# Second layer: scores within groups of four tokens from products on VectorE, summed in 32 by 32 blocks

## The reference, cut to what matters

```
u = rms_norm(h);  q, f, i, gate = split(u @ w_in);  q = silu(q)
f = lb + (1 - lb) * sigmoid(f);  k = 1 - f
S_t = diag(f_t) S_{t-1} + k_t i_t^T;  o_t = S_t^T q_t        (per head)
h + (rms_norm(o) * silu(gate)) @ w_out
```

## Time and profile before

| | |
|---|---|
| median of the runs | 1182.67 us |
| the profiled execution | 1182.29 us |
| its span | 1180.6 us |
| PE busy | 1169.3 us (99%) |
| DVE busy | 784.2 us (66%) |
| ACT busy | 419.6 us (36%) |
| POOL busy | 148.9 us (13%) |

### The profile page before, as it was taken

How to read it: one execution, slowest core, us unless ns; L and a number is a source line. 1 busy time by engine, 2 the same in 40 slices (tenths; PEclk the granted TensorE clock), 3 DMA queues, 4 the chain that set the end, 5 groups by cost and what they waited for, 6 DMA issues and landing times. The chain is left out here.

```text
span 1180.6 us, 20358 instructions
## 1 busy us (share of the span) xinstructions
PE 1169.3 (99%) x7276; PEld 1075.4 (91%) x7276; DVE 784.2 (66%) x1578; ACT 419.6 (36%) x911; POOL 148.9 (13%) x344
## 2 busy tenths in 40 slices
PE   8999999999999999999999999999999999999998
PEld 7999999999999999987888989899999999999787
DVE  5757485757676676773443777878787878688421
ACT  5535353635445444552222232322222322222200
POOL 2421121212030311110004000000000000000000
PEclk9999999999999999999999999999999999999999
DMA  8210223233232301065623111314242321117441
GB/s 249 60 49 19 72 90 108 66 98 90 72 108 73 107 1 46 22 254 188 193 101 90 37 37 44 109 54 144 70 136 77 120 89 38 46 37 295 146 138 72
DMA packets 110657, 113.49 MB, mean 96 GB/s; under 512 B 6880, under 2 KB 86752, under 8 KB 110560
## 3 DMA queue, kind: packets, MB, share of 16 engines
q1 hardware_dynamic: 110560, 112.23, 30.0%
HBM read 79.70 MB, written 32.51 MB: 95 GB/s over the span
## 5 line engine op out<-in xcount | busy, mean ns | idle before, releaser
L28 PE MATMUL p_proj<-w_qkv_hi,ut_hi 128*128 128x384 f32 x504 | 172.0, 341 | 0.2 <-DVE ut_lo L796 0.2
L30 PE MATMUL p_proj<-w_qkv_hi,ut_lo 128*128 128x384 f32 x504 | 169.1, 335 | 0.0
L29 PE MATMUL p_proj<-w_qkv_lo,ut_hi 128*128 128x384 f32 x504 | 168.7, 335 | 0.0
L28 PE MATMUL p_proj<-w_ig_hi,next_hi 128*128 128x256 f32 x512 | 145.6, 284 | 0.0
L29 PE MATMUL p_proj<-w_ig_lo,next_hi 128*128 128x256 f32 x512 | 143.1, 279 | 0.0
L30 PE MATMUL p_proj<-w_ig_hi,next_lo 128*128 128x256 f32 x512 | 143.1, 279 | 0.0
L28 PE MATMUL p_proj<-next_hi,w_qf_hi 128*128 128x512 f32 x282 | 113.2, 402 | 0.0
L30 PE MATMUL p_proj<-next_hi,w_qf_lo 128*128 128x512 f32 x282 | 110.1, 390 | 0.0
L29 PE MATMUL p_proj<-next_lo,w_qf_hi 128*128 128x512 f32 x282 | 109.9, 390 | 0.0
L808 DVE TENSOR_TENSOR_SCAN a_skip<-a_skip,a_diagonal 128x129 f32<-128x129 f32 (+3 forms) x64 | 86.9, 1358 | 30.2 <-ACT a_beta L648 28.4
L29 PEld LDWEIGHTS p_proj<-w_ig_lo,next_hi 128*128 128x128 f32 x512 | 96.3, 188 | 0.0
(11 more groups left out here) (244 smaller groups left out, 2761.6 us busy)
## 6 DMA issues: line engine op xcount, KB each, us to landing
stage<-in_hg_w_in_dram SPq DMA_DIRECT2D x32, 512.0 KB, 4.6
stage<-in_sb_w_in_dram SPq DMA_DIRECT2D x29, 512.0 KB, 5.6
w_out_hi_scratch<-m_in SPq DMA_DIRECT2D x32, 256.0 KB, 2.1
w_out_lo_scratch<-m_in SPq DMA_DIRECT2D x32, 256.0 KB, 2.3
m_in<-mixed_scratch SPq DMA_DIRECT2D x12, 448.0 KB, 5.9
a_beta<-in_x_dram SPq DMA_DIRECT2D x8, 512.0 KB, 4.1
m_in<-in_sb_w_out_dram SPq DMA_DIRECT2D x16, 256.0 KB, 3.5
ut_hi<-w_out_hi_scratch SPq DMA_DIRECT2D x8, 512.0 KB, 8.4
```

The lines of the kernel that those rows point to most:

```text
L28: pe.matmul(out, w_hi, m_hi, start=start, stop=False, skip_group_check=True)
L29: pe.matmul(out, w_hi, m_lo, start=False, stop=False, skip_group_check=True)
L30: return pe.matmul(out, w_lo, m_hi, start=False, stop=stop, skip_group_check=True)
```

## The change

Levels 0 and 1, which hold the scores inside groups of four tokens, no longer go through PE products of keys and queries. At level 0 DVE multiplies the 512 right queries by their left keys, transposes the result in 32 by 32 blocks and sums each block; PE adds the four blocks of features with one product against `same_pair` (`sum_pairs`, 16 columns), and DVE picks one column per tile with a mask, sums it and copies it with the level's mask into the scores. At level 1 the same is done with two products of 512 (one for each query of a pair), a transpose and a sum of 1024, `sum_quads` (32 columns) and two masked copies of 256 elements.

Order: `sum_pairs(n)` stands after `update(h)` at i = 4 (after the projection of use 5 for head 0), `sum_quads(n)` at i = 6 ahead of level 2. On DVE `prepare(n, 1)`, with its products and sums, moves from the start of use 5 to behind `states(h)`, `pick_self_scores` and `place(n, 0)` (not for head 0). The products of level 1 are written into `o`, their transpose into `k_chunk`. The wait of level 3 for level 1 goes. Setup gains the constants `same_half`, `same_pair`, `same_quad`. DVE's steps are written out instead of looped; `splits_rows` is adapted so that the same steps split rows. One semaphore, `folds`, counts all of this. In `finish` one of the two row products of row 6 moves ahead of `turn_outputs`.

The diff, cut to its core:

```diff
-                if level >= 2:
+                if level >= 2 and level != 3:
                     dve.wait_ge(level_done, L * h + level - 1)
-                elif not known_first(h):
+                elif level < 2 and not known_first(h):
...
+                if level == 0:
+                    fold_pairs(h, b, q_out)
+                    return
...
                 dve.wait_ge(prepared, 2 * (L * h + level) + 2)
+                if level == 1:
+                    multiply_quads(h)
                 dve.wait_ge(doubled, 2 * (L * h + level) + 1)
                 dve.tensor_tensor(rights(pre, half), rights(pre, half), left_ends(pre, half),
                                   ALU.mult).then_inc(doubled, 1)
+                if level == 1:
+                    sum_quads_up(h)
+
+            def multiply_quads(h):
+
+                products = flat(o).rearrange("p (m s g r) -> p m s g r", m=TILES, s=2, r=2)
+                keys = k_left[1][:, :].rearrange("p (m g r) -> p m g r", m=TILES, r=2)
+                queries = q_right[1][:, :].rearrange("p (m g s) -> p m g s", m=TILES, s=2)
+                dve.tensor_tensor(products[:, :, 0], keys, queries[:, :, :, 0:1].broadcast_to([P, TILES, BLOCK, 2]),
+                                  ALU.mult)
+                dve.tensor_tensor(products[:, :, 1], keys, queries[:, :, :, 1:2].broadcast_to([P, TILES, BLOCK, 2]),
+                                  ALU.mult).then_inc(folds, 1)
+
+            def sum_quads_up(h):
+
+                if not known_first(h):
+                    dve.wait_ge(k_turned_done, 2 * h)
+                dve.wait_ge(folds, quads_folded(h, 1))
+                dve.transpose(k_chunk[:, :], flat(o)).then_inc(folds, 1)
+                dve.wait_ge(folds, quads_folded(h, 2))
+                dve.tensor_reduce(qk[:, 3 * PARTIALS:4 * PARTIALS], k_chunk[:, :].rearrange("p (n i) -> p n i", i=BLOCK),
+                                  AX.X, ALU.add).then_inc(folds, 1)
+
+            def pick_quads(h):
+                picked = qk[:, 4 * PARTIALS:5 * PARTIALS].rearrange("p (n s) -> p n s", s=2)
+                columns = qk[:, 5 * PARTIALS:5 * PARTIALS + 2 * TILES]
+                dve.tensor_tensor(picked, level_bank(1)[:, :PARTIALS].rearrange("p (n s) -> p n s", s=2),
+                                  same_half[:, :].unsqueeze(1).broadcast_to([P, 2 * TILES, 2]),
+                                  ALU.mult).then_inc(folds, 1)
+                dve.wait_ge(folds, quads_picked(h, 1))
+                dve.tensor_reduce(columns, picked, AX.X, ALU.add).then_inc(folds, 1)
...
+            def fold_pairs(h, b, q_out):
+
+                pre, suf = prefix[b], suffix
+                products, turned = k_left[0], q_right[0]
+                dve.tensor_tensor(q_out, rights(q[b], 1), rights(pre, 1), ALU.mult).then_inc(prepared, 2)
+                dve.tensor_copy(lefts(suf, 1), rights(pre, 1))
+                dve.wait_ge(prepared, 2 * L * h + 2)
+                dve.tensor_tensor(products[:, :].rearrange("p (e b r) -> p e b r", e=2, r=1), q_out, lefts(k[b], 1),
+                                  ALU.mult).then_inc(folds, 1)
+                dve.memset(rights(suf, 1), 1.0).then_inc(doubled, 1)
+                dve.wait_ge(folds, pairs_folded(h, 1))
+                dve.transpose(turned[:, :], products[:, :]).then_inc(folds, 1)
+                dve.wait_ge(doubled, 2 * L * h + 1)
+                dve.tensor_tensor(rights(pre, 1), rights(pre, 1), left_ends(pre, 1), ALU.mult).then_inc(doubled, 1)
+                dve.wait_ge(folds, pairs_folded(h, 2))
+                dve.tensor_reduce(products[:, :PARTIALS // 2], turned[:, :].rearrange("p (n i) -> p n i", i=BLOCK),
+                                  AX.X, ALU.add).then_inc(folds, 1)
...
+                column = pick_pairs(h) if level == 0 else pick_quads(h) if level == 1 else None
                 dve.memset(waits_taken[:, :], 0.0)
                 dve.wait_ge(masks_spread, 2)
+                if level == 0:
+                    whole = score_rows[b][:, :]
+                    dve.copy_predicated(
+                        bass.AP(tensor=whole.tensor, offset=whole.offset + 1,
+                                ap=[whole.ap[0], [HALF - 1, 2], [P, TILES // 2], [2, P // 2]]),
+                        level_mask[:, 0, :].bitcast(I32).rearrange("p (e m b) -> p e m b", e=2, m=TILES // 2),
+                        column.rearrange("p (e m) -> p e m", e=2).unsqueeze(3).broadcast_to(
+                            [P, 2, TILES // 2, P // 2])).then_inc(level_placed, 1)
+                    return
+                if level == 1:
+                    whole = score_rows[b][:, :]
+                    mask = level_mask[:, 1, :].bitcast(I32).rearrange("p (e m g s) -> p e m g s", e=2, m=TILES // 2, s=2)
+                    for side in range(2):
+                        last = dve.copy_predicated(
+                            bass.AP(tensor=whole.tensor, offset=whole.offset + 2 + side,
+                                    ap=[whole.ap[0], [HALF - 2, 2], [P, TILES // 2], [4, BLOCK]]),
+                            mask[:, :, :, :, side],
+                            column[:, :, :, side].unsqueeze(3).broadcast_to([P, 2, TILES // 2, BLOCK]))
+                    last.then_inc(level_placed, 1)
...
-                    if projects and not last_head and i >= 4:
+                    if projects and not last_head and i >= 4 and (i != 5 or known_first(n)):
                         prepare(n, nb, i - 4)
-                    if last_head and i >= 4:
+                    if last_head and i in (4, 6, 7):
                         if i == 7:
                             place(n, nb, 2)
-                        prepare(n, nb, {4: 0, 5: 1, 6: 3, 7: 4}[i])
+                        prepare(n, nb, {4: 0, 6: 3, 7: 4}[i])
                     if last_head and i in (4, 5):
                         split_mixed_lo(dve, m_in, parts, link, i - 4)
                     if mixes and i == 5:
                         states(h, b, p_misc[2:4])
                         pick_self_scores(h, p_misc[2:4])
-                    if last_head and i == 5:
-                        prepare(n, nb, 2)
                     if mixes and i == 6:
                         outputs(h, b)
                     if projects and not last_head and i >= 5:
                         place(n, nb, i - 5)
                     if last_head and i >= 5:
                         place(n, nb, {5: 0, 6: 1, 7: 3}[i])
+                    if projects and i == 5 and not known_first(n):
+                        prepare(n, nb, 1)
+                    if last_head and i == 5:
+                        prepare(n, nb, 2)
...
+            for h in range(-1, HEADS):
+                step(h, h % 2, h >= 0, h < HEADS - 1)
...
-                elif level == 0 and not known_first(h):
-                    pe.wait_ge(last_placed, h)
-                elif level == 1 and not known_first(h):
-                    pe.wait_ge(level_placed, MASKED * h)
...
+            def sum_pairs(h):
+
+                pe.wait_ge(folds, pairs_folded(h, 3))
+                if not known_first(h):
+                    pe.wait_ge(last_placed, h)
+                pe.matmul(level_bank(0)[:, :PARTIALS // 2], same_pair[:, :], k_left[0][:, :PARTIALS // 2],
+                          start=True, stop=True).then_inc(level_done, 1)
+
+            def sum_quads(h):
+
+                pe.wait_ge(folds, quads_folded(h, 3))
+                if not known_first(h):
+                    pe.wait_ge(level_placed, MASKED * h)
+                pe.matmul(level_bank(1)[:, :PARTIALS], same_quad[:, :], qk[:, 3 * PARTIALS:4 * PARTIALS],
+                          start=True, stop=True).then_inc(level_done, 1)
...
+                rows((0,), 6)
                 turn_outputs(h, p_last)
-                rows((0, 1), 6)
+                rows((1,), 6)
...
+                    if i == 5 and known_first(n):
+                        sum_pairs(n)
+                    if projects and i == 6:
+                        sum_quads(n)
+                    if projects and not last_head and i >= 6:
                         multiply_level(n, i - 4)
                     if last_head:
-                        for level in {4: [0], 5: [1], 6: [2, 3], 7: [4]}.get(i, []):
+                        for level in {6: [2, 3], 7: [4]}.get(i, []):
...
+                    if projects and i == 4 and not known_first(n):
+                        sum_pairs(n)
```

More of the change, by code:

```diff
@@ L1581, in splits_rows, with pairs_folded, pairs_picked, quads_folded @@
         def splits_rows(h):
-            return not isinstance(h, int)
-        def self_steps(h, steps):
-            return 4 * h + steps + 2
+            return not isinstance(h, int) or 1 <= h <= HEADS - 4
+        def pairs_folded(h, steps):
+            return 14 * h + 4 + steps + (2 if known_first(h) else 0)
+        def pairs_picked(h, steps):
+            return 14 * h + 9 + steps + (3 if known_first(h) else 0)
+        def quads_folded(h, steps):
```

(47 more changed lines are left out.)

34 lines of the change are left out of this document (19 added, 15 removed).

## The result

The changed kernel takes **1213.40 us** (median of 5 runs, 1213.01 to 1214.03); the kernel before took 1182.97 us beside it (median of 5). The ratio is 1.0256, 95% interval 1.0242 to 1.027: 30.4 us slower. The forecast was 1196.1 us with a range to 1205. The sign was right: it forecast 13.4 us of loss and missed 17.3.

A forecast was written before the change was run, and what follows sets the result against it. TensorE, busy throughout each step, was taken as the bound, with DVE's gated outputs reaching it without slack. Terms 9.6 + 1.0 + 0.5 + 3.3 - 1.0 = +13.4 us on 1182.67 gave 1196.1 us, range 1186 to 1205.

The forecast's parts named there:

- up to step 0's turning: Late DVE makes TensorE wait beyond its saving: +0.5 us in step -1 and +0.5 us in step 0.
- steps 1 to 4: Steps with row splits: DVE ends its gated outputs 2.4 us later in each, +9.6 us in all.
- step 5: Three fewer row splits on DVE's stretch ahead of the gated outputs, so only +0.5 us.
- step 6: TensorE waits 2.4 us for the gate and 2.4 us at level 3, less 1.5 saved: +3.3 us.
- rival 4: TensorE's clock falls in the new pauses, slowing the projections behind: +28 us on the forecast, 1224 us; chance 0.05.
- the placing of level 1: On DVE, two predicated copies of 256 replace one of 512: 0.62 us each, 1.24 us, besides 0.45 for picking.
- rival 2: Each half copy of level 1 costs like today's whole, 1.12 us: 1204 us; chance 0.12.
- TensorE's saving: Small sums replace the products of levels 0 and 1: 12.0 us saved in all, 1.5 us in a step.
- DVE's last stretch before the gated outputs: Turning follows it without slack; 5.8 us added against 3.4 us of idle time ends DVE 2.4 us later.
- the sums and transposes: New DVE work: transpose and sum of 1024 at level 1 take 2.42 us, of 512 at level 0 0.55 each.
- the end's -1.0 us: In the finish, a row product moved ahead fills the last turning's 1.10 us wait: -1.0 us.
- Rivals 1 and 3: 1: repeated-column copies cost 0.34 us each, 1187 us, chance 0.22; 3: DVE's sums fit its spare time, 1169.7 us, chance 0.08.

The follow-up runs named there:

- keep_warm: The changed kernel plus 12 unread identity products on TensorE ahead of turning the outputs in steps 0 to 5; 1203.88 us, ratio 1.0185.
- one_copy: Experiment 6: the changed kernel with level 1's two masked copies of 256 replaced by a spreading plain copy and one masked copy of 512; 1205.23 us, ratio 1.0197.
- pairs_only: The changed kernel with only level 0 in the new way, level 1 made and placed as before; 1176.99 us, ratio 0.9961.
- load_2: The kernel before plus two unread sums of 1024 elements on DVE at use 6 of each step; 1184.92 us, ratio 1.002.
- load_5: The kernel before plus five unread sums of 1024 elements on DVE at use 6 of each step; 1206.57 us, ratio 1.0204.
- relieved: The changed kernel with later row splits, level 1's single copy, one split_lo part behind the gated outputs, step 6's gates ahead of level 1; 1188.55 us, ratio 1.0055.
- relieved_6: As relieved, but step 6's gates stand behind level 1's sums again, as in the changed kernel; 1186.28 us, ratio 1.0036.
- sums_first: The changed kernel with level 1's products and sums back at the start of use 5, ahead of states and placing; 1214.58 us, ratio 1.0268.
- turn_back: The changed kernel with the moved row product of row 6 put back behind the last turning; 1212.76 us, ratio 1.026.
- splits_late: The changed kernel with DVE's row splits moved from uses 3, 4, 6, 7 to 7 and the next step's 0, 1, 2; 1207.49 us, ratio 1.0209.

## Why the prediction was right in kind and wrong in size

The periods, as differences from before in the profiled executions. "Clock kept" is keep_warm.

```
                               forecast   clock kept   changed
up to step 0's turning            +1.0        +2.4        +2.3
steps 1 to 4                      +9.6       +12.3       +19.2
step 5                            +0.5        +1.5        +4.1
step 6                            +3.3        +5.0        +6.6
last turnings to the projection   -1.0        -0.9        -1.0
sum                              +13.4       +20.2       +31.3
```

- **The step that failed is the one that left TensorE's clock out of the sum**: rival 4, with a chance of 0.05. The forecast had the waits (2.0 to 3.9 us a step) and priced each at its own length. Behind each of the pauses ahead of turning half clock cost up to another 2.6 us. The third column over the second is 11.1 us, well over half of the 17.9 us that the sum of the forecast misses (9.5 of 17.3 us in the medians). A rest of it is in step 6 of keep_warm too, which nothing kept warm: its windows 1075 to 1085 and 1085 to 1090 have a clock of 0.89 and 0.88. By an estimate, window length times missing share, 10 x 0.11 + 5 x 0.12, that is up to 1.7 us, about what that step's second column is above its forecast. The rival itself was mis-sized in the other direction, at +28: not a whole projection ran at half clock but a quarter to a half of one. With the 9.5 us in its sum the forecast would have been 1205.6 us. The Trainium skill (TensorE: Matmul & The Clock Gate, "What's actually happening") says that an idle array falls back to half its clock and earns the full one again by work. By that rule, which the forecast cited for rival 4, the clock was a term to weigh; the trace agrees: in steps 0 to 4 0.50 to 0.72 in the five microseconds behind a turning, 0.93 to 1.00 in the next five. No row of before spoke against rival 4, since that TensorE never paused there; a chance of 0.05 had no row behind it.
- **Second, the placing of level 1 was mis-sized**, 1.24 us for a measured 2.11, 0.87 us on each path. It was taken as half of today's copy; experiment 6 shows the price as a term of its own. That was rival 2 (1204 us; that keep_warm took 1203.9 is partly luck, since step 6 of that run holds some half clock too). A warning was in the trace of before: the same 512 elements took 1.32 us at level 0, 1.33 at level 1 and 0.7 at the higher levels, so the time didn't go by the count alone.
- The second column over the first is 0.7 us in each of steps 1 to 4 and 1.0 to 1.7 elsewhere. In steps 1 to 4 DVE sets the period, so there it is the copies' 0.87 us, less some 0.2 by the other terms together.
- **TensorE's saving was a little too high**: 1.3 us a step with the small products in place, not 1.5, and 1.0 in the relieved steps (57.6 - 56.6). Where DVE sets the period this shortens TensorE's waits and not the time.
- **Right**: that DVE's last stretch before the gated outputs has no slack beyond 3.4 us of idle time (pairs_only free, load_2 nearly hidden, load_5 not); that the turning is where it shows; the sums and transposes at 2.41 us; the waits by place, and by length within 0.7 us, in steps -1 to 6; step 6's 2.4 us for the gate.
- **Right in size for a wrong reason**: the end's -1.0 us.
- Rivals 1 and 3 fell: the copy of a repeated column at level 0 costs 1.33 us as before, and the sums do not fit.

What stays open: why a pause of 2.35 to 2.66 us was followed by half clock in some steps and not in others; and exactly how much of step 6's loss is clock, since no run kept it whole there. The same estimate for the change, 5 x (0.08 + 0.26 + 0.34), is up to 3.4 us; the 1.7 by which it is above keep_warm's fits the 1.6 between their columns.

## What to carry to other kernels

Ask of each stall that a change puts into TensorE's stream not only how long it is, but what clock the work behind it gets; where TensorE was never idle before, the old trace can't tell, so give the clock a term of the sum. Filling such a pause with products that nobody reads can be worth more than it costs. Take a change apart by its halves before judging it: here one half fits the idle time and wins, the other half is beyond it and loses about seven times what the first one wins.

## What the runs showed of the hardware

- TensorE's clock by the length of the pause ahead of turning: after 2.00 us or less (six turnings in relieved, six in relieved_6, two in one_copy, two in load_5) it never fell; after 2.95 us (four turnings each in the change, in one_copy, in sums_first and in turn_back, two in splits_late) it always did; in between, at 2.35 to 2.83, both were seen. Where it fell, the ruler lost 1.3 to 2.8 us. These are counts of what was seen and not a rule: length alone doesn't decide, since the clock fell after 2.67 us in the change and after 2.35 in one step of load_5, and stayed after 2.66 in splits_late and after 2.35 in another step of load_5.
- Predicated copies on DVE: 512 elements 0.71 us at the higher levels and 1.33 us at level 0; 256 elements in every fourth place 1.44 us on average. Two of these took 2.11 us from start to start where one of 512 took 1.15 (one_copy).
- The transpose in 32 by 32 blocks of 512 fp32 elements took 0.66 us as a duration and of 1024 1.24 us; a sum of the same inputs 0.67 and 1.22. From start to start the two of 512 took 0.57 and 0.59.
